# First mixer's attention: transposes by row halves, copies on two engines, weighing of twelve pairs on GpSimd

## The reference, cut to what matters

```
s = einsum('bsgrd,bngd->bgrsn', q, k_cmp) * scale          # branch 0: compressed keys
...
s_sel = einsum('bcgrd,bgckd->bcgrk', qc, kg) * scale + bias # branch 1: selected keys
p_sel, den, _ = masked_softmax(s_sel, dist >= 0)
...
o_win, _ = banded_attention(q, kwn, vwn, WIN - 1, 1, rel_bias)  # branch 2: window
o = g[..., 0:1] * o_cmp + g[..., 1:2] * o_sel + g[..., 2:3] * o_win
```

## Time and profile before

| what | value |
|---|---|
| median of 3 runs (lowest to highest) | 1301.36 us (1301.35 to 1302.4) |
| the profiled execution's own time | 1303.89 us |
| its span in the trace | 1301.6 us |
| mean granted TensorE clock | 0.997 |
| PE busy | 1266.0 us, 97% of the span |
| DVE busy | 809.9 us, 62% |
| ACT busy | 642.1 us, 49% |
| POOL busy | 273.0 us, 21% |
| first matmul of the loop to first matmul of `a_out` | 100.24 to 147.11 us |

### The profile page before, as it was taken

The page is one execution under the profiler, slowest core; times in us unless marked ns, Lnnn a source line. Parts: engine busy times, 40 slices in busy tenths (PEclk is TensorE's granted clock), DMA queues, the critical chain, the costliest instruction groups (busy, mean ns, idle before and its releaser), DMA issues.

```text
span 1301.6 us, 19519 instructions
## 1 busy us (share of the span) xinstructions
PE 1266.0 (97%) x7407; PEld 1058.4 (81%) x7407; DVE 809.9 (62%) x1187; ACT 642.1 (49%) x930; POOL 273.0 (21%) x362
## 2 busy tenths in 40 slices
PE   7999999999999999999999999999999999999997
PEld 5986788888799987888888788888887778888886
DVE  3558765555574477654655755556789877755554
ACT  4428654444453366543544645545444683544442
POOL 6420210000000041102000489701177210200000
PEclk9999999999999999999999999999999999999999
DMA  9971545555546654557655565654544436555661
GB/s 285 277 134 22 145 164 193 193 187 181 180 164 193 175 134 131 167 192 181 229 183 176 164 192 192 218 189 143 195 130 150 142 124 200 182 190 193 192 187 40
DMA packets 155883, 224.77 MB, mean 173 GB/s; under 512 B 13395, under 2 KB 107979, under 8 KB 155820
## 3 DMA queue, kind: packets, MB, share of 16 engines
q1 hardware_dynamic: 141008, 208.36, 50.8%
q0 software_dynamic: 10064, 10.54, 4.2%
q10 hardware_dynamic: 4748, 5.02, 1.1%
HBM read 222.56 MB, written 1.25 MB: 172 GB/s over the span
## 4 chain that ended last, share of the span: by engine, by line
PE 80%; DVE 9%; ACT 4%; DMA 3%; issue 2%; POOL 2%; SPq 0%; DVEq 0%; ACTq 0%; POOLq 0%
PE bank L195 23%; PE bank L197 23%; PE bank L196 23%; PE bank L216 4%; DVE units_lo L178 3%; DMA raw_units<-in_a_w_in 2%; PE bank L204 2%; PE bank L702 1%; DMA raw_units<-in_ffn_w_up 1%; ACT arena L1497 1%; DVE arena L3005 1%; PE bank L211 1%; DVE arena L2996 1%; POOL rows L1174 1%; DVE arena L2458 1%
## 5 line engine op out<-in xcount | busy, mean ns | idle before, releaser
L621 DVE TENSOR_TENSOR units_lo<-raw_units,units_hi 128x2048 fp32r<-128x2048 f32 x96 | 222.8, 2320 | 154.4 <-ACT units_hi L575 154.4
L195 PE MATMUL bank<-units_hi,turned_hi 128*128 128x512 f32 (+1 forms) x792 | 307.4, 388 | 3.1 <-DVE units_lo L178 1.3
L197 PE MATMUL bank<-units_hi,turned_lo 128*128 128x512 f32 (+1 forms) x792 | 302.4, 382 | 0.0
L196 PE MATMUL bank<-units_lo,turned_hi 128*128 128x512 f32 (+1 forms) x792 | 301.9, 381 | 0.0
L178 DVE TENSOR_TENSOR units_lo<-raw_units,units_hi 128x2048 fp32r<-128x2048 f32 (+2 forms) x103 | 232.5, 2265 | 107.9 <-ACT units_hi L170 107.6
L170 ACT ACTIVATE units_hi<-raw_units 128x2048 fp32r<-128x2048 f32 (+2 forms) x103 | 193.2, 1886 | 109.8 <-PE bank L197 79.0
L575 ACT ACTIVATE units_hi<-raw_units 128x2048 fp32r<-128x2048 f32 x96 | 183.5, 1912 | 103.8 <-PE bank L197 95.6
L195 PE MATMUL bank<-units_hi,second_hi 128*128 128x512 f32 (+1 forms) x560 | 218.8, 391 | 0.0
L197 PE MATMUL bank<-units_hi,second_lo 128*128 128x512 f32 (+1 forms) x560 | 216.5, 387 | 0.0
L196 PE MATMUL bank<-units_lo,second_hi 128*128 128x512 f32 (+1 forms) x560 | 216.4, 386 | 0.0
L195 PEld LDWEIGHTS bank<-units_hi,turned_hi 128*128 128x128 f32 x792 | 149.3, 188 | 32.8 <-DVE units_lo L178 3.0
(11 more groups left out here) (360 smaller groups left out, 1786.1 us busy)
## 6 DMA issues: line engine op xcount, KB each, us to landing
raw_units<-in_ffn_w_up SPq DMA_DIRECT2D x88, 512.0 KB, 4.8
raw_units<-in_ffn_w_in SPq DMA_DIRECT2D x88, 512.0 KB, 4.7
raw_units<-in_ffn_w_down SPq DMA_DIRECT2D x22, 1024.0 KB, 5.0
raw_units<-in_ffn_w_out SPq DMA_DIRECT2D x22, 1024.0 KB, 5.0
raw_units<-in_w_in SPq DMA_DIRECT2D x18, 1024.0 KB, 5.1
raw_units<-in_b_w_q SPq DMA_DIRECT2D x12, 1024.0 KB, 5.1
raw_units<-in_a_w_in SPq DMA_DIRECT2D x10, 1024.0 KB, 10.2
raw_units<-in_kv_w SPq DMA_DIRECT2D x6, 1024.0 KB, 5.3
```

What stands on the lines that cost most here:

```text
L195: pe.matmul(out, lh, rh, start=start, stop=False, skip_group_check=True)
L196: pe.matmul(out, lh, rl, start=False, stop=False, skip_group_check=True)
L197: return pe.matmul(out, ll, rh, start=False, stop=True, skip_group_check=True)
L621: dve.tensor_tensor(m.WL[:, slot(n0 + j), :], m.RAW[:, slot(n0 + j), :], m.WH[:, slot(n0 + j), :].bitcast(F32), ALU.subtract).then_inc(m.l ...
```

## The change

The turn of a pair becomes twelve transposes of 64 rows by 128 columns, six for rows 0 to 63 into bank 4 and six for rows 64 to 127 into bank 5; each bank then holds a half of the rows of both heads. ACT copies bank 4, DVE copies bank 5. The sums read the turned weights in two strided pieces of 64. For pairs 2 to 13 DVE computes the factor alone and GpSimd does the weighing; these pairs are turned one step later, and the ring of weights holds four pairs, not three. Pairs 0, 1, 14 and 15 stay with DVE.

```diff
-RING_PAIRS = 3
-TURN_AFTER, SUM_AFTER = 2, 3
+RING_PAIRS = 4
+WEIGHED_BY_GPSIMD = range(2, 14)
+TURN_AT = [i + 2 + (i in WEIGHED_BY_GPSIMD) for i in range(NPA)]
+SUM_AT = [t + 1 for t in TURN_AT]
...
+def turn_pair_a_tensor(pe, m, i):
+
+    if i >= 1:
+        pe.wait_ge(m.s("a_turned_copied"), 2 * i)
+    for par in range(2):
+        pe.wait_ge(*weighted_a(m, i, par))
+        for b, at in enumerate((S, 0, P)):
+            for half in range(2):
+                rows = slice(half * DH, (half + 1) * DH)
+                to = (par * 3 + b) * DH
+                ins = pe.transpose(m.pb[4 + half][:, to:to + DH], m.A.PB[rows, i % RING_PAIRS, par, at:at + P],
+                                   m.IDENT[rows, rows])
+                if (par, b) == (1, 2):
+                    ins.then_inc(m.s("a_turned"), 1)
...
+            pt = m.A.PT[:, i % 2, :, :].rearrange("p h (x b q) -> p h x b q", x=2, b=3)[:, :, par, blocks, :]\
+                .rearrange("p h b q -> p b h q")
...
+def attend_a_gpsimd(pool, m):
+
+    for i in WEIGHED_BY_GPSIMD:
+        pool.wait_ge(m.s("a_factor"), 2 * i + 2)
+        for par in range(2):
+            for a, b, tok in HALVES_A:
+                w = m.A.PB[:, i % RING_PAIRS, par, a:b]
+                pool.tensor_scalar(w, w, m.A.RD[:, i, par, tok:tok + 1], None, ALU.mult)\
+                    .then_inc(m.s("a_weighted_by_gpsimd"), 1)
+
+
+def turned_pair_a_vector(dve, m, i):
+
+    dve.wait_ge(m.s("a_turned"), 2 * i + 2)
+    if i >= 2:
+        dve.wait_ge(m.s("a_summed"), 2 * (i - 1))
+    dve.tensor_copy(m.A.PT[:, i % 2, 1, :], m.pb[5][:, 0:3 * P])\
+        .then_inc(m.s("a_turned_copied"), 1)
...
         if 2 < p < NPA + 1:
-            weigh_pair_a_vector(dve, m, p - 1)
+            if p - 1 in WEIGHED_BY_GPSIMD:
+                factor_pair_a_vector(dve, m, p - 1)
+            else:
+                weigh_pair_a_vector(dve, m, p - 1)
+        for i in range(NPA):
+            if TURN_AT[i] == p:
+                turned_pair_a_vector(dve, m, i)
...
             compress_gpsimd(pool, m)
+            attend_a_gpsimd(pool, m)
             pool.wait_ge(m.s("a_biased"), 4 * NPA)
```

More of the change, by code:

```diff
@@ L1389, in score_pair_a_tensor, with weighted_a, sum_pair_a_tensor @@
                 ins.then_inc(m.s("a_scored"), 1)
+def weighted_a(m, i, par):
+    first = WEIGHED_BY_GPSIMD[0]
+    if i in WEIGHED_BY_GPSIMD:
+        return m.s("a_weighted_by_gpsimd"), 4 * (i - first) + 2 * par + 2
+    return m.s("a_weighted"), 4 * (i if i < first else i - len(WEIGHED_BY_GPSIMD)) + 2 * par + 2
+def turn_pair_a_tensor(pe, m, i):
[11 more added lines that the diff above has]
+                    ins.then_inc(m.s("a_turned"), 1)
+def sum_pair_a_tensor(pe, m, i):
+    T, G, r, br = pair_a(i)
+    out = m.pb[6 + T % 2]
+    if i == 0:
+        pe.wait_ge(m.s("cmp_ready"), TT)
+    if br == 0:
+        if T >= 2:
+            pe.wait_ge(m.s("a_out_lo"), T - 1)
+        rr = slice(32 * r, 32 * r + 32)
+        for par in range(2):
+            g = 2 * G + par
+            pe.matmul(out[par * DH:(par + 1) * DH, 0:S], m.A.VCR[rr, g, :], m.A.PCT[rr, g, :], start=True,
+                      stop=False, skip_group_check=True, tile_position=(32 * r, par * DH))
+    pe.wait_ge(m.s("a_turned_copied"), 2 * (i + 1))
+    v = (m.A.VS, m.A.VW)[br]
+    for keys, (a, b) in enumerate(((0, S), (P, S))):
+        for par in range(2):
+            g = 2 * G + par
+            blocks = slice(0, 2) if keys == 0 else slice(2, 3)
+            pt = m.A.PT[:, i % 2, :, :].rearrange("p h (x b q) -> p h x b q", x=2, b=3)[:, :, par, blocks, :]\
+                .rearrange("p h b q -> p b h q")
+            ins = mm(pe, out[par * DH:(par + 1) * DH, a:b].rearrange("p (b h q) -> p b h q", h=2, q=DH),
+                     v[:, keys, g * DH:(g + 1) * DH], pt, False, keys == 1 and br == 1)
+            if keys == 1:
+                ins.then_inc(m.s("a_summed"), 1)
 def attend_a_tensor(pe, m):
     pe.wait_ge(m.s("a_left_out"), 5)
-    for p in range(2, NPA + SUM_AFTER):
+    for p in range(2, SUM_AT[-1] + 1):
         if p < NPA:
@@ L1398, in attend_a_tensor @@
             pe.wait_ge(m.s("a_right_out"), 5)
[L1399 to L1433, removed]
+        for i in range(NPA):
+            if TURN_AT[i] == p:
+                turn_pair_a_tensor(pe, m, i)
+        for i in range(NPA):
+            if SUM_AT[i] == p:
+                sum_pair_a_tensor(pe, m, i)
 def bias_pair_a_vector(dve, m, p):
     T, G, r, br = pair_a(p)
+    if p >= RING_PAIRS:
+        dve.wait_ge(m.s("a_turned"), 2 * (p - RING_PAIRS) + 2)
     for par in range(2):
@@ L1440, in bias_pair_a_vector @@
         dve.wait_ge(m.s("a_scored"), 2 * p + par + 1)
-        if p >= RING_PAIRS:
-            dve.wait_ge(m.s("a_turned"), 2 * (p - RING_PAIRS) + par + 1)
         for a, b, tok in HALVES_A:
@@ L1511, in attend_a_scalar @@
             exp_pair_a_scalar(act, m, p)
[L1512 to L1515, removed]
+        for i in range(NPA):
+            if TURN_AT[i] == p:
+                act.wait_ge(m.s("a_turned"), 2 * i + 1)
                 if i >= 2:
                     act.wait_ge(m.s("a_summed"), 2 * (i - 1))
-                act.activation(m.A.PT[:, i % 2, par, :], m.pb[4 + par][:, 0:3 * P], ACT.Copy)\
+                act.activation(m.A.PT[:, i % 2, 0, :], m.pb[4][:, 0:3 * P], ACT.Copy)\
                     .then_inc(m.s("a_turned_copied"), 1)
```

15 lines of the change are left out of this document (10 added, 5 removed).

## The result

The changed kernel takes **1310.33 us** (median of 5 runs, 1308.66 to 1313.53) against 1302.38 us (5 runs) for the kernel before on the same chip: ratio 1.006, 95% interval 1.0048 to 1.0072, that is 7.9 us slower. The forecast was 1302.0, in a range of 1299.0 to 1306.0.

What follows compares the result with a forecast made beforehand. A ring of waits through PE, ACT and DVE, 6.00 us per two steps, bounds the loop. Gaining 3.16 us in front and losing 3.77 at the end gives +0.6: 1302.0 us, own range 1300.4 to 1303.6, eight in ten 1299.0 to 1306.0.

Steps and rivals of the forecast that it cites:

- The ring and its one shortened piece: Attention loop: waits through PE, ACT and DVE set the pace; only the turn shortens, 0.82 to 0.43, rounds 6.00 to 5.61.
- GpSimd's price, taken as 1.97: Loop: GpSimd weighs a pair in 1.97 us, read from four additions of the same widths, hidden below 2.81 per pair.
- the second rival: Loop: GpSimd sets the pace from 2.81 us per pair on; at 3.34 it adds 6.4, giving 1308.4; chance 0.09.
- The clock, cost at nothing: Loop: PE is busy a smaller share of a round, but its clock stays at 1.00 (2.4 GHz), costing nothing.
- The end, 11.39: Behind the last scores: start of bias(15) to the first projection matmul takes 11.39 us, against 7.62 before.
- GpSimd holds DVE: Loop rival: DVE's factor waits up to 0.66 us for a running weighing; six such waits add 4.0, 1306.0; chance 0.08.
- The rounds fall to the engines' own load: Loop rival: the ring opens, two steps cost PE's 4.75 us, five rounds give 6.25, time 1297.7; chance 0.13.
- After the loop: Behind the loop: nothing changes place; splits, loads and DMAs keep their distance to it.
- half of 0.06: Chance 0.06 of the longer-end rival (1304.5, weighing of pairs 14 and 15 slower); half of it counts as no change.
- slower is 0.20: Whole kernel: chance of being slower by more than 2.6 us, given in the prediction as 0.21.
- the same 0.67: Whole kernel: chance of a time within 2.6 us, about 0.2%, of no change, given in the prediction as 0.66.
- The rule on GpSimd's one-input work: GpSimd's weighing: one-input work runs at about line rate, two-input about twice as slow, so a pair lies below 1.97 us.

Runs made afterwards that it cites:

- e2_quarter: Changed kernel with GpSimd weighing only the first 64 columns of each of its four pieces per pair, the rest unweighed: 1311.77 us, ratio 1.0072.
- e9_fill_quarter: Changed kernel with GpSimd weighing only 64 columns per piece, plus idle-time PE matmuls before the turns of pairs 3, 13, 14 and 15: 1305.9 us, ratio 1.0026.

## Why the prediction was wrong

The projection started 5.90 us later than forecast (153.62 against 147.72). Step by step:

- **The ring and its one shortened piece.** Right; the size was off. Where GpSimd is fast enough the ring sets the pace, 5.73 per round, with the wait for ACT's copy that was forecast. The turn takes 0.51 from its start to PE's next instruction (143.67 to 144.18 after, with a wait ahead of it), not the 0.43 read in the second mixer. bias(5) to bias(15) takes 28.02 in the run with GpSimd's columns cut, forecast 27.30: +0.72, of which the turn's 0.08 makes 0.40 in five rounds; the rest is not traced. bias(5) itself was 0.11 late (109.14).
- **GpSimd's price, taken as 1.97.** Wrong in size, and the wrong row was chosen: an addition of two tensors stood for a product with one factor per row, on the ground that the columns and the neighbours were the same. (Of those 1.97 us only the first 0.46 ran beside the bias, which ended at 1039.99.) The instruction costs 0.94 and 0.61. Its 3.0 to 3.1 per pair lies above the 2.81 from which the second rival was said to decide; that rival's price of 6.4 counted the surplus at 3.34 a pair over twelve pairs from the first on (at 3.0 that count gives 2.3). In the trace it is only 0.90 on bias(15) (28.92 against 28.02), since the first pairs had slack to use up (4.1 us were there for 3.0), and 0.48 at the end, where VectorE's weigh(14) ran beside GpSimd's last pair.
- **The clock, cost at nothing.** The step that failed most: 3.69 of the 5.90. The row behind it (3.44 of 5 busy) has a single wait of PE, 1.53 us, and the clock stayed at 1.00:

```profile
499.64 0.34 PE L1789 MATMUL bank<-ident,arena 64*128 64x64 f32 x4 [1.53 <-ACT rows L1973]
```

  At the loop's end PE is busy 1.92 of 5, with waits of 2.33 and 1.30. The forecast worked out those very waits on PE (its turns stand at 5.46 and later behind bias(15)) and then priced the matmuls behind them at full clock; no rival had the clock in it. The split depends on the order: with the columns cut first, the clock at the end is 4.18 (15.47 in `e2_quarter`, 11.29 in `e9_fill_quarter`) and GpSimd's part there 0.09 in place of 0.48.
- **The end, 11.39.** Right, 11.30 with the clock held and the cheap form, though two small errors offset there: turn(14) 5.22 behind bias(15) for 5.46, from it to the projection 6.08 for 5.93. In the changed kernel itself copy(13) came at 5.01 for 4.85 and turn(14) at 5.61 for 5.46.
- **"GpSimd holds DVE".** Nearly nothing: the factor's second instruction takes 0.37 at most and 0.17 mostly. **"The rounds fall to the engines' own load"** did not happen in any run. **After the loop** the span grew by another 1.6 us in the two profiles; stretches at a lower clock stand in different places of each profile (0.95 in 1000 to 1020 after, 0.94 in 1280 to 1300 before), so what of this belongs to the change stays open. The forecast had everything behind the loop keep its distance.

0.11 + 0.72 + 0.90 + 0.48 + 3.69 is 5.90. One sum of the chances is off as well: half of 0.06 is 0.03, so slower is 0.20 and the same 0.67. The rule on GpSimd's one-input work (the Trainium skill, GPSIMD Engine Reference, "Engine selection", about line rate) was said to put the weighing of a pair below 1.97. For the form that the change uses the runs show the contrary, 0.94 us for 256 columns against 0.61 for two tensors, 3.0 a pair; for the same product with a second factor a pair lies below it, 1.62.

## What to carry to other kernels

When a change makes the matrix engine wait on a path that hangs on it, price what follows at the lower clock too; here waits of 2.3 and 1.3 us were followed by work that took 3.7 us more at the lower clock. Take an engine's price from a row of the same instruction form, not of the same shape. And a gain in front can be lost where the end of the loop must take back the delay that paid for it: look first at what stands behind the last scores.

## What the runs showed of the hardware

- On GpSimd a `tensor_scalar` with one factor per row took 942 ns for 256 columns and 613 ns for 128; with a second operation (times 1.0) 483 and 376; as `tensor_tensor` with a broadcast factor 610 and 396. Why one operation takes longer than two stays open.
- Once an instruction on GpSimd stood still while VectorE split weights. GpSimd and VectorE in the early stretch of the run with four forms:

```profile
82.82 2.86 POOL L1502 TENSOR_SCALAR arena<-arena,parity 128x256 f32<-128x256 f32 x2
```

```profile
83.07 2.37 DVE L178 TENSOR_TENSOR units_lo<-raw_units,units_hi 128x2048 fp32r<-128x2048 f32 x1 [3.25 <-ACT units_hi L170]
```

  The first of the two (256 columns) took 0.49. The second, 128 columns, began at 83.28, behind the split's start, and took 2.40 instead of 0.37: it ended at 85.68, 0.24 behind the split's end at 85.44. The Trainium skill, SBUF — State Buffer, "Who interferes with whom", has a VectorE instruction with two SBUF inputs contend with a GpSimd instruction that reads SBUF, over a port pair that one of them holds exclusively; this row agrees.
- A wait of 1.7 us on PE ahead of turn(1) was followed by a granted clock of 0.50 in seven of eleven profiles in which it stood, and in neither of the two in which matmuls filled it. What decides between the eleven is not settled. At the loop's end, where nothing filled waits of 1.7 to 2.3 us and a second one behind them, it was 0.50 in all five profiles that had them; behind the single wait of 1.53 us in the second mixer before it stayed at 1.00.
